# Rotary turn of queries and keys: from TensorE and VectorE to GpSimd

## The reference, cut to what matters

```python
q = rms_norm(q) * gain                     # over the features of one head
first, second = halves of the head's features
q = concat(first * cos - second * sin,     # RoPE
           second * cos + first * sin)
```

## Time and profile before

| | us |
|---|---|
| median of 3 runs | 2406.17 (2405.64 to 2407.56) |
| the profiled execution | 2404.93 |
| its span in the trace | 2402.9 |
| stage AB, from its first tile to the last | 769 to 972 |
| stage C, from its first product to the barrier | 1780 to 1881 |
| one turn's product on TensorE, 30 records for 15 turns (L1177) | 0.59 each |
| VectorE busy over the span | 1256.2 |
| GpSimd busy over the span | 971.3 |
| TensorE busy over the span | 2294.7 |

### The profile page before, as it was taken

The page is one execution under the profiler, slowest core; times in us unless marked ns, Lnnn a source line. Parts: engine busy times, 40 slices in busy tenths (PEclk is TensorE's granted clock), DMA queues, the critical chain, the costliest instruction groups (busy, mean ns, idle before and its releaser), DMA issues. The chain is left out here.

```text
span 2402.9 us, 34322 instructions
## 1 busy us (share of the span) xinstructions
PE 2294.7 (95%) x14079; PEld 1901.2 (79%) x14079; DVE 1256.2 (52%) x2102; ACT 802.1 (33%) x1406; POOL 971.3 (40%) x639
## 2 busy tenths in 40 slices
PE   6999989999998999988999999999999998999999
PEld 5876757778776789965888888888886787888887
DVE  3647468756646660679155695755349651411111
ACT  4434353332325312456132121211143463322222
POOL 1336325555552222326234352534422123645653
PEclk8999989999999999989999999999999999999999
DMA  8335235535543111000111434343112002323321
GB/s 272 108 101 181 88 106 185 170 115 162 171 145 116 36 53 61 29 1 1 53 54 53 141 106 141 105 141 106 53 62 71 19 1 71 105 88 106 103 77 47
DMA packets 227577, 228.31 MB, mean 95 GB/s; under 512 B 7439, under 2 KB 225507, under 8 KB 227427
## 3 DMA queue, kind: packets, MB, share of 16 engines
q1 hardware_dynamic: 227091, 226.09, 29.4%
q10 hardware_dynamic: 336, 0.11, 0.0%
HBM read 224.08 MB, written 2.10 MB: 94 GB/s over the span
## 5 line engine op out<-in xcount | busy, mean ns | idle before, releaser
L1628 POOL TENSOR_TENSOR w_lo<-ring,w_hi 128x1024 fp32r<-128x1024 f32 x124 | 303.8, 2453 | 353.8 <-ACT w_hi L1622 353.8
L2598 DVE SCALAR_TENSOR_TENSOR xT<-ps,mods,xT 128x512 f32<-128x512 f32 (+1 forms) x160 | 107.7, 682 | 464.7 <-PE ps L1703 430.2
L1622 ACT ACTIVATE w_hi<-ring 128x1024 fp32r<-128x1024 f32 x124 | 130.7, 1058 | 490.9 <-PE ps L1703 490.9
L1701 PE MATMUL ps<-hidden_hi,w_hi 128*128 128x512 f32 (+1 forms) x768 | 272.6, 355 | 0.6 <-POOL hidden_lo L2986 0.6
L2889 DVE SCALAR_TENSOR_TENSOR ffn_sums<-ps,cols,ffn_sums 128x441 f32<-128x441 f32 (+2 forms) x352 | 214.9, 687 | 109.4 <-ACT ffn_sums L2808 109.4
L1702 PE MATMUL ps<-hidden_lo,w_hi 128*128 128x512 f32 (+1 forms) x768 | 272.0, 354 | 0.0
L1703 PE MATMUL ps<-hidden_hi,w_lo 128*128 128x512 f32 (+1 forms) x768 | 271.7, 354 | 0.0
L1701 PE MATMUL ps<-h_hi,w_hi 128*128 128x512 f32 (+1 forms) x720 | 255.5, 355 | 0.0
L1702 PE MATMUL ps<-h_lo,w_hi 128*128 128x512 f32 (+1 forms) x720 | 255.0, 354 | 0.0
L1703 PE MATMUL ps<-h_hi,w_lo 128*128 128x512 f32 (+1 forms) x720 | 254.7, 354 | 0.0
L2831 POOL TENSOR_TENSOR ffn_w_lo<-ring,ffn_w_hi 128x1024 fp32r<-128x1024 f32 (+2 forms) x76 | 161.7, 2129 | 215.9 <-ACT ffn_w_hi L2781 215.9
(11 more groups left out here) (477 smaller groups left out, 5192.0 us busy)
## 6 DMA issues: line engine op xcount, KB each, us to landing
ring<-in_mlp_w SPq DMA_DIRECT2D x64, 1024.0 KB, 5.4
ring<-in_ada_w SPq DMA_DIRECT2D x48, 1024.0 KB, 5.4
ring<-in_w_ada SPq DMA_DIRECT2D x24, 1024.0 KB, 5.3
ring<-in_ffn_w_up SPq DMA_DIRECT2D x22, 1024.0 KB, 5.2
ring<-in_ab_w_in SPq DMA_DIRECT2D x11, 1024.0 KB, 5.3
ring<-in_ffn_w_down SPq DMA_DIRECT2D x12, 768.0 KB, 4.7
ring<-in_w_in SPq DMA_DIRECT2D x8, 1024.0 KB, 8.8
ring<-in_c_w_in SPq DMA_DIRECT2D x6, 1024.0 KB, 5.0
```

Source lines behind the costliest of these rows:

```text
L1622: act.activation(w_hi[m][:, 0:x["kt"], :], ring[:, x["n"] % NS, 0:x["kt"], m * P:(m + 1) * P], ACT.Copy).then_inc(SW["w_hi"].sem, 1)
L1628: pool.tensor_tensor(w_lo[m][:, 0:x["kt"], :], ring[:, x["n"] % NS, 0:x["kt"], m * P:(m + 1) * P], w_hi[m][:, 0:x["kt"], :].bitcast(F32), ...
L1701: pe.matmul(o, w_hi[m][:, k, :], h, start=(k == 0), stop=False)
L2598: return nc.vector.scalar_tensor_tensor(x, bank, column_of(gates, t * 2 + 2 * gate + r), x, ALU.mult, ALU.add)
```

## The change

The matrices `ROT32` and `ROT64` and the function `rope` (which nothing calls) go. In `units_stage` the turn is GpSimd's: for each run of 32 (AB) or 64 (C) partitions one product of the tile's other half with the sine, read from shifted partitions, and then the whole tile times cos and the sum. The sine table carries the sign, for the partition that is read. Each instruction waits for the one before it (`g_order.step`). TensorE's products L1177 and VectorE's L1186 to L1189 are gone, with their semaphores.

```diff
-(IDENT, ONES, TINY, BLK64, U_LE, U_GE, ROT32, ROT64, SWAP, M_PREV, M_NEXT, DFT_C, DFT_S, SEL) = range(14)
+(IDENT, ONES, TINY, BLK64, U_LE, U_GE, SWAP, M_PREV, M_NEXT, DFT_C, DFT_S, SEL) = range(12)
...
-        t[n], t[n + 1] = np.cos(ang), np.sin(ang)
+        t[n], t[n + 1] = np.cos(ang), np.where(i[:, None] % head < head // 2, 1, -1) * np.sin(ang)
...
-            def rotations(pe, n):
-                for u, src in rot_lots[n]:
-                    i = rot_no[u]
-                    head_wait(pe, "head_normed", u + 1)
-                    if i >= 2:
-                        pe.wait_ge(R_["rot_sin"].sem, R_["rot_sin"].at(i - 1))
-                    pe.matmul(ps[:, (4, 7)[i % 2], :], mats[:, rot_mat, :], src, start=True, stop=True)\
-                      .then_inc(R_["rot"].sem, 1)
-
-            def rotated(dve, n):
+            def rotated(pool, n, lows):
                 if tables is not None and n == 0:
-                    dve.wait_ge(mats_in, tables_at[0])
+                    pool.wait_ge(mats_in, tables_at[0])
                 for u, t in rot_lots[n]:
-                    i = rot_no[u]
-                    dve.wait_ge(R_["rot"].sem, R_["rot"].at(i + 1))
-                    v_order.step(dve, dve.tensor_tensor(t, t, cos, ALU.mult))
-                    dve.tensor_tensor(rot_tmp, ps[:, (4, 7)[i % 2], :], sin, ALU.mult).then_inc(R_["rot_sin"].sem, 1)
-                    dve.wait_ge(R_["rot_sin"].sem, R_["rot_sin"].at(i + 1))
-                    v_order.step(dve, dve.tensor_tensor(t, t, rot_tmp, ALU.add))
+                    head_wait(pool, "head_normed", u + 1)
+                    pool.wait_ge(n_lo.sem, n_lo.at(lows))
+                    for p0 in range(0, P, half):
+                        p1 = p0 + half if p0 // half % 2 == 0 else p0 - half
+                        g_order.step(pool, pool.tensor_tensor(rot_tmp[p0:p0 + half, :], t[p1:p1 + half, :],
+                                                        sin[p1:p1 + half, :], ALU.mult))
+                    g_order.step(pool, pool.tensor_tensor(t, t, cos, ALU.mult))
+                    g_order.step(pool, pool.tensor_tensor(t, t, rot_tmp, ALU.add))
...
                     for h in range(ahead, n_halves):
                         low(pool, h)
+                        if h >= 7 and h % 2 and (h - 7) // 2 < len(rot_lots):
+                            rotated(pool, (h - 7) // 2, h + 1)
+                    for n in range(max(0, (n_halves - 6) // 2), len(rot_lots)):
+                        rotated(pool, n, n_halves)
...
                 if (n, m) == (4, 0):
                     self.wait(pe, "gate_logs", 1)
-                    pe.wait_ge(S["rot_sin"].sem, S["rot_sin"].at(4))
                     self.lot(pe, (0, 1), 0, NLAT, (0, 0))
...
                 heads(dve, 1)
-                rotated(dve, 0)
-                rotated(dve, 1)
                 heads(dve, 2)
...
                 self.wait(dve, "gate_kinds", 8)
-                rotated(dve, 2)
                 self.rows(dve)
```

More of the change, by code:

```diff
@@ L68, in shape_constants @@
     m[U_GE] = i[:, None] >= i[None, :]
[L69 to L72, removed]
     m[SWAP] = np.roll(np.eye(P), 64, axis=0)
@@ L1108, in units_stage @@
         def units_stage(slab0, units, norm, narrow, bias_rows, cleared=(), ada=None,
-                        on_dve=None, on_act=None, head_jobs=(), head_mat=None, head=P, post=None, w_low=None, lead=None, gates=None, turn=None, narrow_to=None, tables=None, parts_ahead=False, paced=(), rot_at={}):
+                        on_dve=None, on_act=None, head_jobs=(), head_mat=None, head=P, post=None, w_low=None, lead=None, gates=None, turn=None, narrow_to=None, tables=None, parts_ahead=False, paced=()):
             jobs_of = [[] for _ in units]
@@ L1157, in head_roots @@
                                    scale=1.0 / head).then_inc(H["head_std"].sem, 1)
-            R_ = named("rot", "rot_sin")
-            rot_no, rot_lots = {}, []
+            rot_lots = []
             if turn is not None:
[L1162 to L1167, removed]
@@ L1168, in units_stage @@
-            assert len(rot_after) == sum(1 for x in rot_lots if x)
-            rot_late = sum(len(x) for x in units) - 2 if None in rot_after else None
-            def rotations(pe, n):
-                for u, src in rot_lots[n]:
-                    i = rot_no[u]
-                    head_wait(pe, "head_normed", u + 1)
-                    if i >= 2:
-                        pe.wait_ge(R_["rot_sin"].sem, R_["rot_sin"].at(i - 1))
-                    pe.matmul(ps[:, (4, 7)[i % 2], :], mats[:, rot_mat, :], src, start=True, stop=True)\
-                      .then_inc(R_["rot"].sem, 1)
@@ L1180, in rotated @@
-            def rotated(dve, n):
+                half, cos, sin, rot_tmp = turn
+                rot_lots = [[(u, src) for u, (src, m, _) in js if m == LAT] for js in jobs_of]
+            def rotated(pool, n, lows):
                 if tables is not None and n == 0:
-                    dve.wait_ge(mats_in, tables_at[0])
+                    pool.wait_ge(mats_in, tables_at[0])
                 for u, t in rot_lots[n]:
-                    i = rot_no[u]
-                    dve.wait_ge(R_["rot"].sem, R_["rot"].at(i + 1))
-                    v_order.step(dve, dve.tensor_tensor(t, t, cos, ALU.mult))
-                    dve.tensor_tensor(rot_tmp, ps[:, (4, 7)[i % 2], :], sin, ALU.mult).then_inc(R_["rot_sin"].sem, 1)
-                    dve.wait_ge(R_["rot_sin"].sem, R_["rot_sin"].at(i + 1))
-                    v_order.step(dve, dve.tensor_tensor(t, t, rot_tmp, ALU.add))
+                    head_wait(pool, "head_normed", u + 1)
[6 more added lines that the diff above has]
+                    g_order.step(pool, pool.tensor_tensor(t, t, rot_tmp, ALU.add))
@@ L1202, in head_norm @@
                     heads(dve, n)
[L1203 to L1206, removed]
             stride = 3 if ada else 1
@@ L1350, in _ @@
                             gates.pe(pe, n, m)
[L1351 to L1354, removed]
                         if fresh_slab and n == 1 and narrow is not None:
@@ L1378, in _ @@
                     if gates is not None:
-                        gates.dve(dve, heads, rotated)
+                        gates.dve(dve, heads)
                     else:
@@ L1490, in units_stage @@
                 x.close(n_jobs)
-            for x in R_.values():
-                x.close(len(rot_no))
             if ada:
@@ L2169, in convolve, with dve @@
                             ins.then_inc(S["conv_done"].sem, 1)
-            def dve(self, dve, heads, rotated):
+            def dve(self, dve, heads):
                 v_order.step(dve, dve.scalar_tensor_tensor(t_a, dt, -1.0, dt, ALU.mult, ALU.max))
@@ L3088, in head_norms @@
                 R[n].close(len(jobs))
[L3090 to L3112, removed]
         def attention(jobs, scale, bufs, made):
@@ L3556, in pe @@
                     self.wait(pe, "gate_rows", 1)
-                    pe.wait_ge(S["rot_sin"].sem, S["rot_sin"].at(5))
                     for d in range(2):
@@ L3678, in program @@
                     rows[:, GATE_B:GATE_B + 16], head_jobs=head_jobs, head_mat=blk64, head=64, post=post, gates=gates,
-                    turn=(ROT32, rope_tabs[:, 0, :], rope_tabs[:, 1, :], ada_rows[:, 0:LAT]), narrow_to=kb[0:32, 0, :], paced=(1,), rot_at={1: (3, 2), 2: (4, 3)},
+                    turn=(32, rope_tabs[:, 0, :], rope_tabs[:, 1, :], ada_rows[:, 0:LAT]), narrow_to=kb[0:32, 0, :], paced=(1,),
                     tables=(rope_tabs, w["const_tables"][T_CB:T_CB + 2].rearrange("t p n -> p t n")))
@@ L4005, in program @@
         units_stage(W["c"], units, c_norm, None, None, parts_ahead=True,
-                    head_jobs=head_jobs, head_mat=ones, turn=(ROT64, tabs[:, 0, :], tabs[:, 1, :], ada_rows[:, 0:LAT]),
+                    head_jobs=head_jobs, head_mat=ones, turn=(64, tabs[:, 0, :], tabs[:, 1, :], ada_rows[:, 0:LAT]),
                     tables=(tabs, w["const_tables"][T_CC:T_CC + 2].rearrange("t p n -> p t n")))
```

## The result

| | us |
|---|---|
| kernel before, median of 6 runs | 2407.31 (2405.64 to 2410.91) |
| changed kernel, median of 6 runs | 2417.73 (2414.97 to 2419.49) |
| ratio | 1.004, 95% interval 1.0029 to 1.0051 |
| profiled execution of the changed kernel, its span | 2418.49, 2416.5 |

The changed kernel is slower, by 9.6 us of 2407 as the ratio has it (7.0 to 12.3). Predicted were 2420 us and a range of 2405 to 2430.

What follows compares the result with a forecast made beforehand. TensorE was taken to fill AB, with VectorE's chain ending late, and VectorE's last turn to end C. 10.4 + 1.3 + 2.5 = 14.2 us on 2402.9, plus 2.03 and 1.24, gave 2420 us; range 2405 to 2430.

Steps and rivals of the forecast that it cites:

- What ends stage C: Stage C, ahead of attention's barrier: GpSimd's run of turns and low parts ends last, at 1891.6 against VectorE's 1881.23.
- 1.3 us whatever the partitions: GpSimd's turns in AB and C: each 512-column instruction takes 1.295 us on 32, 64 or 128 partitions, shifted or not.
- Rivals A and C: GpSimd's turns: A, fewer partitions shorten instructions, 2398 us, chance 0.09; C, shifted reads double them, about 2470 us, chance 0.07.
- The pushes in C: Stage C: eight VectorE gain products each delay GpSimd's run by 0.67 us, 5.4 us in all.
- +10.4: Stage C: GpSimd's run ends at 1891.6 instead of VectorE's 1881.23, delaying the barrier by 10.4 us.
- The clock: Attention's opening: TensorE, after standing still over ten us, runs at a lower granted clock, costing 1.3 us, between 0 and 2.6.
- the hold-up: Stage AB: VectorE's row chain alternates with GpSimd's instructions and loses 9 to 10 us, its nine us of lead.
- the term that no row before could show: Stage AB: chain scans wait for GpSimd's instructions, giving +2.5 us; without that for scans, -4 to -5.
- a push on top of it: Stage AB: one chain instruction of 1.75 us delays GpSimd further, so low 13 ends near 883.6, against 881.9 before.
- +2.5: Stage AB's net loss in us, from low 13 and the chain's end moving back; bounds -5 and +8.
- Rival B: Both stages: hold-ups do not add up, C +5.0 and AB -5, no change, 2406 us; chance 0.16.
- The sum: Whole kernel: 10.4 for C, 1.3 for the clock and 2.5 for AB make 14.2 us on the span of 2402.9.

Runs made afterwards that it cites:

- the first kernel of the experiments: Changed kernel with GpSimd making only stage AB's turns, stage C as before the change: 2407.10 us, ratio 0.9997 (0.9987 to 1.0006) to the kernel before.

## Why the prediction was right, and where its terms were off

**What ends stage C: right.** GpSimd's run replaced VectorE's, and took attention with it. The end at 1892.91 is 1888.4 counted from low 7, which lies 4.5 us later in this execution; predicted was 1891.6.

**1.3 us whatever the partitions: right.** Rivals A and C fall with one answer, on the shifted products (shortest, median, longest in ns, both shapes 20 times):

```profile
L1168 POOL TENSOR_TENSOR ada_rows<-big x40: 1256/1285/2689, 818.8 to 1889.0; 32x512 f32<-32x512 f32 x20, 64x512 f32<-64x512 f32 x20
```

The products and sums on 128 partitions, which are not shifted, have a median of 1.288 us; so 32, 64 and 128 partitions all take 1.29 us, shifted or not. By the Trainium skill, GPSIMD Engine Reference, "2.1 Instruction dispatch", each core works on its own 16 partitions; the trace agrees in that fewer partitions did not shorten the instruction.

**The pushes in C: less than half as big.** This is the step of the prediction that failed. It let each gain product of VectorE push GpSimd back by the product's whole duration less the gap, 8 x 0.67 = 5.4 us. VectorE's first gain product in GpSimd's run, beside GpSimd's sum:

```profile
1829.91 1.15 DVE L1179 SCALAR_TENSOR_TENSOR big<-big,cols,rstd 128x512 f32<-128x512 f32 x1
1830.99 3.34 DVE L1177 RECIPROCAL mean<-mean 128x512 f32<-128x512 f32 x1
```

It waits for GpSimd's product (1829.23 to 1830.52) and ends at 1831.06; the sum of 1830.60 takes 1.62 instead of 1.29. So GpSimd loses 0.33 us and not 0.67: I had counted the gain product's whole duration as time in which the other is shut out. The GpSimd rows beside the eight gain products are 0.22 to 0.33 us longer than others of their shape, 2.3 us in all. With 2.3 in place of 5.4 the predicted run is 54.8 + 9.6 + 2.3 = 66.7 us, and 66.6 are measured from low 7's end; so +10.4 was +7.1.

**The clock: right in kind, +2.0 instead of +1.3,** within the bounds of 0 and 2.6.

**AB: the hold-up right, what it delays wrong.** The chain's start was predicted at 857.7 and came at 857.75 by the old count. The scans are held up: those of 768 columns take 3.22, 2.77 and 2.67 us, where the earlier trace rows has 1.75, and the last, of 512 columns, takes 3.34, where it took 1.25 before:

```profile
876.40 1.25 DVE L3650 TENSOR_TENSOR_SCAN big<-big 4x512 f32<-4x512 f32 x1
```

That is the term that no row before could show. By the Trainium skill, SBUF — State Buffer, "Who interferes with whom", a VectorE instruction with two SBUF inputs contends with a GpSimd instruction that reads SBUF; by this trace scans do too. The hold-up is 8.2 us, 9 to 10 were predicted. What failed is the step behind it: lot 2 and a push on top of it were to delay low 13 to an end at 883.6. The pushes were too big here as well. Lot 2 was to last from about 861 to 877, 16 us, of which its own instructions are 8.2; it lasted 12.4 (862.48 to 874.87). So low 12 was over at 875.7 by the old count, low 13 waited for its high part and not for GpSimd, and the chain's 0.9 us of lead went through: low 13 ended near 880.9, ahead of the 881.9 of before, and not behind it as the prediction's sign had it. +2.5 was -0.9, within the bounds of -5 and +8; the first kernel of the experiments has AB at -0.7 (-3.1 to +1.4).

**Rival B had half a point:** the pushes were smaller than the forecast's. But scans and gain products did wait, the eight gain products for up to 2.23 us as predicted, and C's +7.1 and the clock's 2.0 are far from even.

**The sum.** 7.1 + 2.0 - 0.9 = 8.2 us by rows, against 14.2 predicted; the medians are 10.4 apart, 7.0 to 12.3 by the interval. (The two profiled executions are 13.6 apart; the other 5.4 lie ahead of low 5 of AB, 3.0, and between the two stages, 2.4, where the change does nothing.) That 2420 came within 2.3 us of 2417.73 is in part luck, because a second error had the other sign: the execution that I took the terms from lay 1.24 us below the median of three runs, but 2.4 below that of six. 2404.93 + 8.2 + 2.4 is 2415.5; the 2.2 us left to the median are less than the runs of one kernel scatter, and I assign them to nothing.

## What to carry to other kernels

An engine that stands idle on average is not free where the work is moved to: lay the moved work end to end from the moment its input is there, and compare its end with the old one. All ten turns ran 7 us over GpSimd's room in C. Six of ten fitted, but gained nothing there with two lots ahead of the next low parts (59.9 us, 60.0 before) and 5.0 us with one. Behind which low part a lot stood was worth 5 to 6 us by the medians, in AB and in C (2.9 and 5.0 in the traces), since whatever is queued behind it on an in-order engine waits too. Where two engines hold each other up, look for the serial chain of the other engine that lies beside the moved work, and move the work behind it.

## What the runs showed that I had not expected

- A push is smaller than the instruction that pushes. VectorE's eight gain products in C took 1.00 to 2.23 us beside an unbroken run of GpSimd, 0.75 with GpSimd idle, and each cost GpSimd 0.22 to 0.33 us.
- VectorE's reciprocal is not longer in that run: 3.34 us for 512 columns at 1830.99, beside three GpSimd instructions in a row, and 3.34 before the change at 1822.03, with GpSimd idle.
- The order of two GpSimd instructions that depend on each other costs 0.08 us whether the second reads other partitions or the same; a turn's four instructions of C took 5.35 us (1882.29 to 1887.64), and shifting the partitions added nothing to them.
